# Two MLPs in two phases: half of the up projections by seven products, the inner activations kept in DRAM

## The reference

```python
u = rmsnorm(h, norm_mlp_g[l]) @ w_up[l]          # 1024x1024 @ 1024x4096
h = h + jnp.square(jax.nn.relu(u)) @ w_down[l]   # 1024x4096 @ 4096x1024
```

## Time and profile before

| | us |
|---|---|
| median of 3 runs | 3121.2 |
| profiled execution, device time | 3119.3 |
| its span, first to last instruction | 3117.5 |
| PE busy, share of the span | 3039.6, 98% |
| DVE busy | 1906.4, 61% |
| POOL busy | 1213.1, 39% |
| ACT busy | 830.9, 27% |
| mean granted PE clock | 0.994 |

### The profile page before, as it was taken

One profiled execution on the slowest core, in us unless ns is written; L12 is line 12 of the kernel. 1 busy time (PEld: TensorE's weight loads), 2 busy tenths in 40 slices (PEclk: granted clock), 3 DMA queues, 4 the chain that ended last, 5 costly groups with the idle time before them and its releaser, 6 DMA issues.

```text
span 3117.5 us, 38588 instructions
## 1 busy us (share of the span) xinstructions
PE 3039.6 (98%) x14694; PEld 2411.0 (77%) x14694; DVE 1906.4 (61%) x1975; ACT 830.9 (27%) x1161; POOL 1213.1 (39%) x1071
## 2 busy tenths in 40 slices
PE   7999999998999999999999999999999999999997
PEld 6776667885878888888767777887678788888886
DVE  7988874435357777773556565221776577777724
ACT  3005772114221111112243435112652211111111
POOL 3334332330334555553323333333453355555550
PEclk9999999999999999999999999999999999999999
DMA  3111002130111111111312121422221111111121
GB/s 141 48 41 34 2 28 81 48 128 1 47 41 53 49 55 54 54 48 48 115 51 81 51 81 61 155 79 77 100 115 54 41 55 55 48 55 55 48 68 54
DMA packets 50110, 194.62 MB, mean 62 GB/s; under 512 B 5680, under 2 KB 6320, under 8 KB 48560
## 3 DMA queue, kind: packets, MB, share of 16 engines
q1 hardware_dynamic: 43776, 152.50, 14.6%
q10 hardware_dynamic: 6192, 40.14, 3.4%
HBM read 171.12 MB, written 21.50 MB: 62 GB/s over the span
## 4 chain that ended last, share of the span: by engine, by line
PE 87%; DVE 8%; ACT 2%; issue 1%; DMA 1%; POOL 1%; SPq 0%; ACTq 0%; DVEq 0%; POOLq 0%
PE psum L489 56%; PE psum L746 15%; PE psum L924 3%; DVE cacc L1426 2%; PE psum L799 2%; PE psum L572 2%; PE psum L586 2%; PE psum L601 2%; PE psum L860 1%; PE psum L874 1%; PE psum L847 1%; PE psum L715 1%; DVE rstd L1413 1%; DMA raw<-weights 1%; PE psum L695 1%
## 5 line engine op out<-in xcount | busy, mean ns | idle before, releaser
L383 POOL TENSOR_TENSOR small<-ident 128x1 f32<-128x1 f32 x202 | 54.7, 271 | 1380.1 <-PE psum L489 1246.7
L489 PE MATMUL psum<-A_hi,w_hi 128*128 128x512 f32 x1792 | 562.9, 395 | 21.7 <-DVE A_lo L1403 13.6
L489 PE MATMUL psum<-A_lo,w_hi 128*128 128x512 f32 x1792 | 553.5, 390 | 0.0
L489 PE MATMUL psum<-A_hi,w_lo 128*128 128x512 f32 x1792 | 553.1, 390 | 0.0
L389 POOL TENSOR_TENSOR w_lo<-raw,w_hi 128x1024 fp32r<-128x1024 f32 x186 | 482.9, 2596 | 15.5
L489 PEld LDWEIGHTS psum<-A_hi,w_hi 128*128 128x128 f32 x1792 | 336.6, 189 | 102.3 <-issue 30.7
L489 PEld LDWEIGHTS psum<-A_lo,w_hi 128*128 128x128 f32 x1792 | 337.4, 188 | 70.8
L489 PEld LDWEIGHTS psum<-A_hi,w_lo 128*128 128x128 f32 x1792 | 337.3, 188 | 70.5
L489 PE MATMUL psum<-B_hi,w_hi 128*128 128x512 f32 x1088 | 337.8, 392 | 4.5 <-DVE t L1672 2.9
L489 PE MATMUL psum<-B_hi,w_lo 128*128 128x512 f32 x1088 | 335.5, 390 | 0.0
L489 PE MATMUL psum<-B_lo,w_hi 128*128 128x512 f32 x1024 | 315.8, 390 | 0.0
(11 more groups left out here) (273 smaller groups left out, 4389.6 us busy)
## 6 DMA issues: line engine op xcount, KB each, us to landing
raw<-weights SPq DMA_DIRECT2D x256, 512.0 KB, 3.3
gate_spill<-RU SPq DMA_DIRECT2D x16, 512.0 KB, 3.1
H<-x ACTq DMA_DIRECT2D x2, 2048.0 KB, 8.5
x_spill<-H ACTq DMA_DIRECT2D x1, 4096.0 KB, 11.1
R<-gate_spill ACTq DMA_DIRECT2D x8, 512.0 KB, 4.5
mixed_spill<-t ACTq DMA_DIRECT2D x8, 512.0 KB, 2.9
BE<-rel_bias ACTq DMA_DIRECT2D x8, 512.0 KB, 4.5
MIX<-mixed_spill ACTq DMA_DIRECT2D x1, 4096.0 KB, 14.3
```

The lines of the kernel that those rows point to most:

```text
L489: last = pe.matmul(PJ[s][:, c:c + step], w[:, s, k, :], b[:, k, c:c + step], start=(k == 0 and i == 0), stop=(k == kblocks - 1 and i == 2))
```

## The change

The units are now: two ups, eight **fast** pairs of up units, six groups of two ups and four downs, two ups, eight lasts.

- **fast_up**: a pair of up tiles is made by seven products of 12 matmuls (84 for 96), on 2x2 blocks: two halves of the 1024 input features by two output tiles by two halves of tokens. Three products take the input as it is, four take sums of it (`SX`), made once for the MLP by ACT and DVE from `H` (`copies`, `input_sums`, `input_low`). The weight sums of a fast pair (`WSX`, 128x512 each) are made by DVE (for the first pair by POOL); POOL splits seven operands into four slots `WX`. DVE combines the seven banks in `TT2` (T[0] and T[1] together), ACT copies, squares and stores them.
- **hid0, hid1** are DRAM tensors. 30 of the 32 squared inner tiles are stored there, the other two stay on the chip. A group's four tiles are loaded back by SP into the low half of `XS` (as `XSF`), block by block as the last pair of the group before is done with them.
- **combine** now makes one operand for a whole group: four sums and seven low parts of 128x1024 on DVE, seven high parts on ACT. The first pair of a group waits product by product (`st_lo`).
- The weight sums of the down pairs (`WS`, four of 128x256) are made by POOL in front of `split_pair`, no longer by DVE.

```diff
-    units = [("up", t) for t in range(4)]
+    units = [("up", 0), ("up", 1)]
+    units += [("fast", 2 * n + 2 + i) for n in range(FAST) for i in range(2)]
+    t = 2 * FAST + 2
     for g in range(GROUPS):
-        units += [("up", 4 * g + 4), ("up", 4 * g + 5)] + [("down", g, j) for j in range(4)]
-        if g < GROUPS - 1:
-            units += [("up", 4 * g + 6), ("up", 4 * g + 7)]
-    return units + [("up", t) for t in range(26, 32)] + [("last", m) for m in range(KB)]
+        units += [("up", t), ("up", t + 1)] + [("down", g, j) for j in range(4)]
+        t += 2
+    return units + [("up", t), ("up", t + 1)] + [("last", m) for m in range(KB)]
...
+            def load_hidden(layer, g, q):
...
+                sp.dma_start(x[:, 0, 1, :, :], hid[:, :, 0, 0:HALF]).then_inc(S["hx_a"], 16)
+                sp.dma_start(x[:, 1, 1, :, :], hid[:, :, 1, 0:HALF]).then_inc(S["hx_c"], 16)
...
+                    sp.wait_ge(S["st_done"], 4 * pair + 4)
+                sp.dma_start(x[:, 5, 1, :, :], hid[:, :, 0, HALF:SEQ]).then_inc(S["hx_b"], 16)
+                if g:
+                    wait_job(sp, q - 2, 1)
+                sp.dma_start(x[:, 2, 1, :, :], hid[:, :, 1, HALF:SEQ]).then_inc(S["hx_d"], 16)
...
+            def split_fast(q, layer, n):
...
+                for p in range(7):
+                    before = 7 * n + p - 4
...
+                        wait_product(pool, layer, before // 7, before % 7)
+                    if p == 2 and n:
+                        pool.wait_ge(S["st_weights"], (FAST - 1) * layer + n)
...
+                    chain(pool.tensor_scalar(hi, w, 1.0, 1.0, ALU.mult, ALU.mult))
+                    pool.tensor_tensor(lo, w, f32(hi), ALU.subtract).then_inc(S["us_split" if p < 5 else "w_split"], 1)
+
+            def weight_sums(q, s):
+
+                pool.wait_ge(raw_in[s], 16 * q + 16)
+                k = lambda a: raw[:, s, 2 * a:2 * a + 2]
+                to = lambda a: WS[:, 2 * a:2 * a + 2, :]
+                chain(pool.tensor_tensor(to(0), k(2), k(3), ALU.add))
+                pool.tensor_tensor(to(2), k(0), k(2), ALU.subtract)
+                chain(pool.tensor_tensor(to(1), to(0), k(0), ALU.subtract))
+                chain(pool.tensor_tensor(to(3), k(1), to(1), ALU.subtract))
...
+                    weight_sums(q, s)
                     split_pair(q, s, layer)
-                    pairs += 1
-                    pool.wait_ge(S["st_weights"], 4 * GROUPS * layer + pairs)
...
+            def fast_up(q, layer, n, x, norm):
...
+                    if p == 1 and n:
+                        pe.wait_ge(S["us_read"], made)
+                    if p == 2:
+                        pe.wait_ge(free[1], q)
+                    if p == 4:
+                        pe.wait_ge(free[0], q)
+                    if n == 0 and p > 2:
+                        pe.wait_ge(S["st_lo"], SPLITS * layer + 2 * (p - 2))
...
+                for n_fast in range(FAST):
+                    t = 2 * n_fast + 2
+                    wait_product(act, layer, n_fast, 0)
+                    for part in range(2):
+                        act.wait_ge(S[f"hid{part}"], 16 * (STORES * layer + n_fast + 1))
...
+                    tallies["us_copied"](act.activation(TT2[:, :, 0:HALF], twice, ACT.Copy))
+                    for half, side in enumerate(("left", "right")):
+                        act.wait_ge(S["us_" + side], FAST * layer + n_fast + 1)
+                        part = TT2[:, :, half_of(half)]
+                        chain(act.activation(part, part, ACT.Square))
+                        act.dma_start(hid[:, t:t + 2, half_of(half)], part).then_inc(S[f"hid{half}"], 16)
...
+                def fast_up(n):
...
+                    tl["us_read"](dve.tensor_tensor(TT2[:, :, left], PX[:, 1024:2048].rearrange("p (a b) -> p a b", a=2),
+                                                    TT2[:, :, left], ALU.add))
+                    chain(dve.tensor_tensor(T[0][:, right], PJ[1][:, 0:HALF], T[1][:, left], ALU.add))
+                    wait_product(dve, layer, n, 4)
+                    chain(dve.tensor_tensor(T[1][:, right], PJ[0][:, 0:HALF], T[1][:, left], ALU.add))
+                    if n + 1 < FAST:
+                        weight_sums(n + 1)
+                    wait_job(dve, q, 0)
+                    dve.tensor_tensor(T[1][:, left], PJ[0][:, HALF:SEQ], T[1][:, right], ALU.add).then_inc(free[0], 1)
+                    dve.wait_ge(free[0], q + 1)
+                    evict_half(0, "us_left")
+                    wait_job(dve, q, 1)
+                    dve.tensor_tensor(TT2[:, :, right], twice(PJ[1][:, HALF:SEQ]), TT2[:, :, right], ALU.add).then_inc(free[1], 1)
+                    dve.wait_ge(free[1], q + 1)
+                    evict_half(1, "us_right")
...
+                    def lows(*order):
+                        for i in order:
+                            dve.wait_ge(S["st_hi"], high + (1, 2, 3, 4, 5, 7, 6)[i])
+                            minus(tl["st_lo"], x[:, i, 1], part(i), f32(x[:, i, 0]))
...
+                    minus(tl["st_sum"], part(3), part(5), part(0))
+                    lows(0)
+                    dve.wait_ge(S["hx_d"], 16 * (GROUPS * layer + g) + 16)
+                    minus(tl["st_sum"], part(4), part(2), part(5))
+                    minus(tl["st_sum"], part(6), part(2), part(3))
+                    dve.wait_ge(S["hx_c"], 16 * group + 16)
+                    minus(tl["st_sum"], part(5), part(1), part(6))
+                    lows(1, 6)
...
+                    evict(q, 0)
+                    lows(4, 5, 2, 3)
+                    stored(1, before)
+                    evict(q, 1)
```

358 lines of the change are left out of this document (248 added, 110 removed).

## The result

The changed kernel takes 3171.65 us (median of 4 runs, 3170.01 to 3173.78), the kernel before 3121.31 on the same chip (4 runs, 3117.48 to 3123.01): a ratio of 1.0163, 95% interval [1.0146, 1.0181], 50.3 us slower. The forecast was 3184, in a range of 3112 to 3206. The profiled execution has a span of 3169.3 us, 51.8 above the 3117.5 of before. Of all runs in this document one was slow (3400.1 us at a mean granted clock of 0.846, one of the ten of experiment 3), and the ratio given there leaves it out.

What follows compares the result with a forecast made beforehand. It took TensorE's matmuls (busy 98%) as the bound. Per MLP, -21.8 for removed matmuls, +15.0 for the fast stage and +38 for groups, twice, gave +62.4 and 3184 us; range 3112 to 3206.

Steps and rivals of the forecast that it cites:

- Term 2: Down pairs: four weight sums on POOL at 0.80 us each make a POOL pair 10.7 us against PE's 9.52.
- Term 3: Down groups: DVE and POOL exclude each other; 11 delays of 0.85 make a group 66.2, costing 38 us per MLP.
- 1 matmuls removed: MLPs: 96 fewer matmuls in each take off 21.8 us per MLP, 43.5 in all, if PE stays fed.
- Term 4: Start of the fast stage: late input sums and low parts cost 7.2, a late bank 6.8; 14.0 us per MLP.
- Term 5: Fast pairs after the start: pairs take 19.7 against PE's 19.04, 0.6 over six times, 3.9 us per MLP.
- old stall: Before the change, reciprocal and rebase left PE one gap of 2.87 us, subtracted from the new losses.
- Term 6: Stores, loads, last products and the rest: cost nothing; eighth low part due 9.5 us after the last up.
- Rival B: POOL's short sums take near 0.60 us without DVE beside them, so no change: 3119; chance 0.09.
- the ring of T: Fast pairs: evict, square, store, copy, DVE work and evictions form a cycle of 19.7 us, 0.6 over PE's 19.04.
- Rival C: Fast pairs: stores land late, at 6 us the ring is 20.4 and both MLPs lose 5 each: 3194; chance 0.10.
- Rival A: Groups: DVE's and POOL's operations fit between each other, under 3.4 us of delay a group: 3091, faster; chance 0.17.

Runs made afterwards that it cites:

- experiment 3: Changed kernel with POOL's down-pair weight sums cut to 16 of 128 columns, except each MLP's first; output not the reference's: 3119.07 us, ratio 0.9988.
- kernel 1: Changed kernel with the down pairs' weight sums moved back from POOL to DVE: 3129.78 us, ratio 1.0026.
- kernel 9: From kernel 5, the second eviction and second pair's sums put ahead of the last two low parts (2, 3): 3126.47 us, ratio 1.0007.
- experiment 2: Changed kernel with DVE's combine sums and low parts cut to 32 of 1024 columns (first group's sums whole); output not the reference's: 3114.61 us, ratio 0.9972.
- experiment 4: Changed kernel with DVE's rebase of H moved from before the first fast pair's additions to behind the fourth fast pair: 3167.37 us, ratio 1.0146.
- experiment 6: From kernel 5, a new order of ACT, DVE and POOL work at the start of the fast stage: 3121.72 us, ratio 0.9996.
- experiment 7: From the kernel of experiment 6, the rebase of H moved behind the first fast pair: 3118.63 us, ratio 0.9986.
- experiment 10: From kernel 9, with experiment 6's start order and the rebase in two halves, behind the first and second fast pairs: 3118.38 us, ratio 0.9991.
- kernel 5: From kernel 1, with the down pairs' sums on DVE put earlier for a group's first two pairs: 3125.97 us, ratio 1.0008.

## Why the prediction was right, point by point

The sign, the mechanism of the groups (terms 2 and 3) and most of the size held: +62 forecast, +50 measured. That the sum came so near is luck in part, since errors of both signs lie in it. By its terms, us for one MLP, measured from one matmul's start to the next's in the first and the second MLP:

| term | forecast | measured |
|---|---|---|
| 1 matmuls removed | -21.8 | -21.8, -21.8 (192 fewer in all) |
| 2, 3 six groups | +38 | +29.1, +29.1 |
| 4 start of the fast stage | +14.0 | +16.0, +16.9 |
| 5 fast pairs after it | +3.9 | +1.6, +1.7 |
| first up job behind them waits for POOL | not in it | +2.1, +2.1 |
| old stall gone | -2.9 | -4.8, -4.8 |
| 6 last products | 0 | 0, +0.9 |
| 6 outside the MLPs, both together | 0 | +5.2 |

The rows of one MLP add up to +22.2 and +24.1, where its stretch grew by 22.4 and 24.2.

**Term 2 was mis-sized: a weight sum takes 0.74 us, not 0.80.** Tile WS in the changed kernel, and parts of POOL's timeline in one group:

```profile
L529 POOL TENSOR_TENSOR WS<-raw x48: 731/740/1741, 1060.6 to 3020.0; 128x256 f32<-128x256 f32 x48
...
L551 POOL TENSOR_TENSOR w_lo<-WS,w_hi x48: 2365/2391/3236, 1075.5 to 3027.8; 128x1024 fp32r<-128x1024 f32 x48
```

```profile
1124.10 1.72 POOL L529 TENSOR_TENSOR WS<-raw 128x256 f32<-128x256 f32 x1
1125.90 1.61 POOL L530 TENSOR_TENSOR WS<-raw 128x256 f32<-128x256 f32 x1
...
1134.00 2.14 POOL L494 TENSOR_TENSOR W<-raw,W 128x512 fp32r<-128x512 f32 x1
1136.22 1.75 POOL L495 TENSOR_TENSOR W<-raw,W 128x256 fp32r<-128x256 f32 x1
1138.06 1.91 POOL L550 TENSOR_SCALAR w_hi<-WS 128x1024 fp32r<-128x1024 f32 x1
1140.05 3.21 POOL L551 TENSOR_TENSOR w_lo<-WS,w_hi 128x1024 fp32r<-128x1024 f32 x1
...
1154.48 0.73 POOL L529 TENSOR_TENSOR WS<-raw 128x256 f32<-128x256 f32 x1
...
1157.62 0.19 POOL L489 TENSOR_TENSOR small<-ident 128x1 f32<-128x1 f32 x1
...
1160.34 0.74 POOL L495 TENSOR_TENSOR W<-raw,W 128x256 fp32r<-128x256 f32 x1
...
1164.78 0.74 POOL L529 TENSOR_TENSOR WS<-raw 128x256 f32<-128x256 f32 x1
```

From 1154.48 to 1164.78 a pair is 10.30, where 10.7 was forecast. The difference is in the four sums, 3.14 from 1154.48 to 1157.62 where 3.52 was forecast: 0.24 of it is the shorter operations, and the rest is that one of the gaps of 0.08 is not there. Four times 0.4 is 1.6, and the forecast group of 66.2 less 1.6 is 64.6: 64.56 was measured. The prices that the prediction gives for other sizes of a sum are too steep: an MLP has 96 of them, so 0.10 less for each takes off at most 9.6 us, and not the 13 between its 38 and its 25. The 0.80 of the earlier trace rows was the same within 5 ns in all 48 cases, which was taken as a sign that nothing disturbed them. It was no such sign: the same operation (L495) takes 0.74 here, where the sums are no longer DVE's. In kernels 1 and 9, with the sums back on DVE, it takes 0.80 and 0.81 again when they run beside it. Rival B had this right in kind, and its 0.60 was too low.

**Term 3 held to a tenth of a microsecond in this group.** POOL's operations from 1124.10 to 1143.34 exceed what they take alone by 0.98, 0.87, 0.98, 0.87, 0.46, 0.86, 0.85, 1.01, 0.86, 0.82 and 0.87, 9.4 in all, as forecast (11 of 0.85); over the twelve groups the sum is 8.7 to 9.7. DVE's begin later than forecast, 3.8 us after the last pair instead of 1.5, since its loads take 6.0 us to land and not 3.3 to 4.5: by then the up split is through, and the sums are held in its place. That changed which operations wait, and hardly how many: ten or eleven in each group. That both the exclusion and POOL's longer pairs are needed is shown by experiments 2 and 3; that moving the sums to POOL is what brought the loss by experiment 1. The rule of the Trainium skill ("SBUF — State Buffer", the part on its two sides) that the shared pair is an exclusive lock fits all of these rows, and so does its word that ACT has ports of its own: ACT's copies took 1.06 in every kernel.

**Term 4 was near in sum and wrong in its parts.** PE in the first fast pairs (start us, us):

```profile
896.01 1.19 PE L911 MATMUL psum<-SX,WX_hi 128*128 128x512 f32 x2 [4.61 <-DVE SX L1846]
...
897.43 1.05 PE L911 MATMUL psum<-SX,WX_hi 128*128 128x512 f32 x2
...
907.35 0.70 PE L911 MATMUL psum<-SX,WX_hi 128*128 128x512 f32 x2 [0.51 <-DVE SX L1846]
...
922.11 0.76 PE L911 MATMUL psum<-A_hi,WX_hi 128*128 128x512 f32 x1 [4.59 <-DVE TT L1911]
```

The fourth product was late by 4.6 (forecast 3.8). The next two were forecast to wait 1.1 each for DVE, and did not: PE itself was slow and used the time up. The last waited 0.51. Windows of 4 us there, the clock in the third column from the end:

```profile
892.00:896.00 4.00, 0.00 (x0) 0.02 (x1) 2.77 (x3) 2.94 (x3) 3.92 (x3) 0.79 0.00 0
896.00:900.00 4.00, 3.99 (x10) 3.13 (x11) 3.93 (x3) 2.31 (x3) 3.92 (x3) 0.50 0.09 17
900.00:904.00 4.00, 4.00 (x17) 3.26 (x16) 3.93 (x3) 0.00 (x0) 3.72 (x4) 0.85 0.66 245
904.00:908.00 4.00, 3.50 (x16) 2.63 (x15) 3.93 (x3) 0.00 (x0) 3.92 (x3) 1.00 0.00 0
```

During the 4.6 us without work the granted clock fell to the lower of its two levels, 1.2 GHz, and matmuls were 0.427 apart instead of 0.227 until about 901. From 896.01 to 907.35, less the 0.51 of waiting, 36 matmuls took 10.8 us instead of 8.2, and after the second wait the 12 from 922.11 took 4.19 instead of 2.72: 4.1 us in all, on top of 4.61 + 0.51 + 1.44 + 4.59 = 11.15 of waiting. The forecast had no term for it. The old stall had it too: behind its wait of 2.87 us seven matmuls were 0.43 apart, and from start to start it cost 4.8 in all, so 4.8 and not 2.9 was given back. The Trainium skill ("TensorE: Matmul & The Clock Gate", Part 1) says that an idle array falls to half its clock; the trace agrees, 0.427 against 0.227.

**Term 5 came near by luck.** It had each of six fast pairs 0.6 late by the ring of T, 3.9 us. The third to the seventh pair of the first MLP take 19.04, 19.04, 19.23, 19.64 and 19.41, and with the eighth the ring cost 1.6. Another 2.1, which the forecast had nowhere, is the wait of the first up job behind them for POOL. POOL begins the split at 1050.6, 2.4 before its product is due, and the low part takes 3.21 instead of 2.39 with DVE's eviction beside it:

```profile
1055.16 0.73 PE L600 MATMUL psum<-A_hi,w_hi 128*128 128x512 f32 x2 [1.97 <-POOL w_lo L458]
```

**Rival C** did not come, though its sign showed in part: stores landed in 2.7 at the median, 9 of the 60 took 4.3 to 4.9, and ACT's copy waited longer than 3.5 for them in 5 of 14 cases, at most 4.9. Rival A needed less than 3.4 us of delay per group, and there were 9.4.

**Term 6 was wrong by about 6 us.** 0.9 of it is in the last products of the second MLP: the first of them waits 1.13 for the eighth low part of its input, where it waited 0.21 before. The forecast had this part due 9.5 us after the last up; in the second MLP a product takes half of the tokens, and it is due after 4.8. Then 5.2 lie between the MLPs, over half of them here. PE, after a wait of 1.85 where the kernel before had 0.54, by windows of 4 us:

```profile
2340.00:2344.00 4.00, 2.83 (x13) 2.02 (x11) 3.41 (x3) 1.06 (x1) 3.92 (x2) 1.00 0.00 0
2344.00:2348.00 4.00, 3.31 (x8) 2.61 (x9) 3.77 (x3) 1.06 (x1) 3.92 (x4) 0.62 0.38 131
```

Of the rest about 1.5 are in the neighbourhood attention, with a clock of 0.50 in the 4 us from 2200, against 1.00 in the same place before, and 0.7 at a wait for DVE at 1740. In the other twelve profiles of changed kernels the stretch between the MLPs is 2.6 to 5.4 us longer than before. Why that wait was longer, and why the attention's short waits cost the clock in one kernel and not in the other, was not tried.

Not foreseen was what experiments 4, 6, 7 and 10 met: that an idle stretch of DVE is not free, if POOL is busy in it. Experiments 4 and 6, costed by DVE's time first of all, gave a third and a half of what was expected; experiment 7, costed with POOL's delay in it, gave what was expected.

## What to carry to other kernels

Where two engines exclude each other, as DVE's operations with two SBUF inputs and POOL's do here, cost an operation by both: its own time, and what it does to the other engine at the place where it will land; an idle stretch of the one is worth nothing while the other is the late one. Two costs that each fit into the slack may break it together, so test them one at a time. And add to a wait of TensorE that lasts some microseconds what its clock may take afterwards, here 1.4 to 2.7 us behind waits of 2.9 to 4.6. It is not sure for shorter ones: the same wait of 1.97 us behind the fast pairs cost 0.1 more in the first MLP and 1.7 more in the second.

## What the runs showed of the hardware that was not expected

- POOL's two-input operation of 128x256 takes 0.74 us with DVE quiet, 0.80 with DVE's short sums about; 128x32 takes 0.26.
- A DVE operation of 128x2048 on two SBUF tensors held POOL's 0.62 us operation to 2.66, 2.0 more, where one of 128x1024 adds 0.8 to 1.0. The size of the pieces matters, beside the number of them.
- Loads of 512 KB in which each piece is 2 KB long (`XSF<-hid`) took 6.0 us to land, the weights' 3.3 and the stores 2.7. The first two of a group are issued 0.4 us apart and are under way together; whether that or the pieces make the difference was not tried.
- The same stretch of the same code can run at either pace after the same wait. At the program's start PE's matmuls are 0.43 apart in kernels 1 and 9. After a wait of 1.36 us in both they came in pairs 0.46 apart in kernel 1, and still 0.85 apart for 5 us in kernel 9:

```profile
17.40 0.74 PE L598 MATMUL psum<-A_hi,w_hi 128*128 128x512 f32 x2 [1.36 <-POOL w_lo L458]
17.98 0.63 PE L598 MATMUL psum<-A_lo,w_hi 128*128 128x512 f32 x2
18.44 0.62 PE L598 MATMUL psum<-A_hi,w_lo 128*128 128x512 f32 x2
```

```profile
17.80 1.22 PE L598 MATMUL psum<-A_hi,w_hi 128*128 128x512 f32 x2 [1.36 <-POOL w_lo L458]
18.82 1.05 PE L598 MATMUL psum<-A_lo,w_hi 128*128 128x512 f32 x2
19.68 1.05 PE L598 MATMUL psum<-A_hi,w_lo 128*128 128x512 f32 x2
```

The recorded clock of that stretch is 1.00 in both, so here the spacing tells it and the record doesn't. Over the thirteen profiles of changed kernels the first MLP's statistics matmul begins between 870.3 and 875.4 us, after code that no edit touched. With what lies between the MLPs, and with the fast stages of kernels 1, 5 and 9, which are alike in code and take 172.8, 170.6 and 173.5 us in the first MLP, that makes several microseconds which belong to no edit. Medians a few us apart, as those of kernels 1 and 5, 5 and 9 or 7 and 10, don't rank them; a stage time in the trace does only if the stage is the one that was edited and shows the change in more than one place.
